# Feed-forward gate: silu and its scaling move from SBUF and GpSimd into PSUM and to VectorE

## What is computed

```python
def swiglu(x, w_in, w_out):
    gate, up = jnp.split(x @ w_in, 2, axis=-1)
    return (jax.nn.silu(gate) * up) @ w_out

x = x + 0.5 * swiglu(rms_norm(x, norm_g[l, 0]), ffn_w_in[l, 0], ffn_w_out[l, 0])
```

## Time and profile before

| | |
|---|---|
| three runs, median | 2074.32 us (2071.76 to 2074.66) |
| profiled execution, first to last instruction | 2071.8 us |
| profiled execution, its own time | not given apart from the span |
| TensorE busy | 2041.6 us, 99% |
| VectorE busy | 1329.3 us, 64% |
| ScalarE busy | 867.2 us, 42% |
| GpSimd busy | 1297.1 us, 63% |
| mean granted TensorE clock | 0.995 of full speed |

### The profile page before, as it was taken

The page is one execution under the profiler, slowest core; times in us unless marked ns, Lnnn a source line. Parts: engine busy times, 40 slices in busy tenths (PEclk is TensorE's granted clock), DMA queues, the critical chain, the costliest instruction groups (busy, mean ns, idle before and its releaser), DMA issues.

```text
span 2071.8 us, 41329 instructions
## 1 busy us (share of the span) xinstructions
PE 2041.6 (99%) x16420; PEld 1994.5 (96%) x16420; DVE 1329.3 (64%) x1873; ACT 867.2 (42%) x1651; POOL 1297.1 (63%) x999
## 2 busy tenths in 40 slices
PE   9999999999999999999999999999999999999998
PEld 8999999999989999999999999999998799999997
DVE  7861884425756882497578439844876678816853
ACT  6641662121574661364256226511432446505631
POOL 6775777654425676677767757765643267766773
PEclk9999999999999999999999999999999999999999
DMA  4321333122112232223123322333210232322231
GB/s 158 102 105 69 103 110 122 65 103 71 68 43 92 82 111 92 76 101 125 69 82 103 112 66 99 117 112 112 88 62 31 90 102 82 118 77 101 93 123 45
DMA packets 31702, 190.61 MB, mean 92 GB/s; under 512 B 3888, under 2 KB 6448, under 8 KB 13104
## 3 DMA queue, kind: packets, MB, share of 16 engines
q1 hardware_dynamic: 24192, 173.43, 24.3%
q10 hardware_dynamic: 7344, 14.89, 2.0%
HBM read 180.81 MB, written 7.50 MB: 91 GB/s over the span
## 4 chain that ended last, share of the span: by engine, by line
PE 52%; DVE 20%; POOL 10%; ACT 8%; issue 6%; DMA 2%; ACTq 0%; DVEq 0%; POOLq 0%; SPq 0%
PE ps L615 36%; PE ps L630 8%; DVE tg L2362 5%; POOL sil L526 4%; DVE tg L2359 4%; POOL ws L507 3%; DMA wraw<-in_wf_in 2%; POOL wl L573 2%; DVE a L2271 2%; DVE s L2300 2%; ACT sil L1761 2%; DVE ps L2280 2%; ACT ps L1692 1%; ACT ws L1725 1%; DVE ps L2338 1%
## 5 line engine op out<-in xcount | busy, mean ns | idle before, releaser
L690 PE MATMUL ps<-tt,ws 128*128 128x272 f32 x3840 | 526.2, 290 | 7.2 <-DVE ws L2304 6.4
L690 PEld LDWEIGHTS ps<-tt,ws 128*128 128x128 f32 x3840 | 500.0, 189 | 10.7 <-DVE ws L2304 7.3
L615 PE MATMUL ps<-a,wh 128*128 128x272 f32 x3028 | 500.3, 287 | 1.6 <-POOL wl L573 1.6
L573 POOL TENSOR_TENSOR wl<-wraw,wh 128x512 fp32r<-128x512 f32 (+1 forms) x351 | 475.2, 1376 | 12.7
L569 POOL TENSOR_SCALAR wh<-wraw 128x1024 fp32r<-128x1024 f32 (+2 forms) x152 | 167.7, 1103 | 471.2 <-PE ps L615 244.7
L615 PEld LDWEIGHTS ps<-a,wh 128*128 128x128 f32 x3028 | 423.6, 188 | 3.7 <-POOL wl L573 3.4
L690 PE MATMUL ps<-u,ws 128*128 128x272 f32 x2880 | 401.6, 288 | 1.1 <-DVE tg L2350 0.6
L507 POOL TENSOR_TENSOR ws<-wraw,ws 128x512 fp32r<-128x512 f32 x240 | 330.9, 1391 | 99.1 <-ACT ws L1700 55.6
L690 PEld LDWEIGHTS ps<-u,ws 128*128 128x128 f32 x2880 | 376.6, 188 | 2.4 <-issue 1.6
L615 PE MATMUL ps<-a,wl 128*128 128x272 f32 x1514 | 311.9, 287 | 0.0
L507 POOL TENSOR_TENSOR ws<-s,ws 128x512 fp32r<-128x512 f32 x160 | 209.0, 1306 | 142.3 <-ACT ws L1725 142.3
(11 more groups left out here) (391 smaller groups left out, 2929.4 us busy)
## 6 DMA issues: line engine op xcount, KB each, us to landing
wraw<-in_wf_in SPq DMA_DIRECT2D x87, 1024.0 KB, 4.8
wraw<-in_wf_out SPq DMA_DIRECT2D x32, 1408.0 KB, 6.0
wraw<-in_w_ab SPq DMA_DIRECT2D x12, 1024.0 KB, 4.8
wraw<-in_w_cd SPq DMA_DIRECT2D x10, 1024.0 KB, 4.9
wraw<-in_w_abo SPq DMA_DIRECT2D x8, 512.0 KB, 3.6
wraw<-in_w_cdo SPq DMA_DIRECT2D x8, 512.0 KB, 3.6
wraw<-in_w_bv SPq DMA_DIRECT2D x2, 1024.0 KB, 4.9
out_y<-yout ACTq DMA_DIRECT2D x14, 136.0 KB, 1.9
```

The lines of the kernel that those rows point to most:

```text
L573: piece = nc.gpsimd.tensor_tensor(wl[:, s, some], wraw[:, par_, s * K * P + some.start: s * K * P + some.stop], wh[:, s, some].bitcast(F32 ...
L615: last = nc.tensor.matmul(bank(b0 + 2 * s + half, 0, HT), w[:, s, k * P:(k + 1) * P], act_t[:, k0 + k, part, half * HT:(half + 1) * HT], s ...
L690: last = nc.tensor.matmul(bank(b, 0, HT), ws[weights][w][:, i * P:(i + 1) * P], moving[:, part], start=(start and i == 0 and w == 0 and pa ...
```

## The change

Silu is written by ScalarE into two banks of PSUM that its period no longer needs (banks 3 and 4 for b = 0, 0 and 1 for b = 1: the F and X bank of the period), not into `sil`. VectorE multiplies it there by `rstd` (`gate_scale`, in place) where GpSimd did so in SBUF, waits for its own completion (`link`), and `glu` reads the gate from PSUM. GpSimd's instruction is gone; so is VectorE's line 2392, whose place `gate_scale(end)` takes. The X bank is now in use until the last product, so `evac[0]` is given by that product instead of by ScalarE's copy, the copy gives a new semaphore `row_copied`, and the second output product waits for `evac[0]`. Each `glu` keeps its order: right half, C22 of the end period where there is one, left half. `link` (line 2114) adds a semaphore increment to an instruction and makes VectorE wait for it.

```diff
--- before.py
+++ after.py
@@ -360,8 +360,9 @@
         a21_in, w_sum, near_high, far_high = sem("a21_in"), sem("w_sum"), sem("near_high"), sem("far_high")
         sum_split, mix_split = sem("sum_split"), sem("mix_split")
         seven_done, t3_ready = sem("seven_done"), sem("t3_ready")
-        snap_ready, c_ready, silr_ready, snap_free = (
-            sem("snap_ready"), sem("c_ready"), sem("silr_ready"), sem("snap_free"))
+        snap_ready, c_ready, snap_free, row_copied = (
+            sem("snap_ready"), sem("c_ready"), sem("snap_free"), sem("row_copied"))
+        GATE_PAIR = [3, 0]
 
 
 
@@ -406,6 +407,7 @@
                 chains.append([Period(first + i, SEVENS * f + i - LEAD, i, DC, (hi - 1 - i) % 2, i == hi - 1)
                              for i in range(lo, hi)])
             SEQ.append(chains)
+        PAIR_OF = {(f, p.i): p.c for f in range(4) for chain in SEQ[f] for p in chain}
 
 
         ORDER, ORDER_END = ["P1", "P5", "P6", "P2", "P7"], ["P1", "P6", "P5", "P7", "P2"]
@@ -521,9 +523,6 @@
                     pool.wait_ge(far_high, 3 * p.q + 2)
                     pool.wait_ge(w_sum, 4 * p.q + 4)
                     low(p, A22, quarter(p, 3)).then_inc(w_split[1], 1)
-                    if last:
-                        pool.wait_ge(sil_done, FC * f + last.i + 1)
-                        nc.gpsimd.tensor_tensor(sil[:], sil[:], rstd[:], ALU.mult).then_inc(silr_ready, 1)
                     pool.wait_ge(far_high, 3 * p.q + 3)
                     low(p, S4, s34[:, 1, 0:p.K * P // 2]).then_inc(mix_split, 1)
 
@@ -902,6 +901,7 @@
 
                 _, c0, c1, _, K = STAGE[stage]
                 product(0, c0, K, a, act_ready, base, early=1)
+                pe.wait_ge(evac[0], c0)
                 product(1, c1, K, a, act_ready, base)
                 run(stage, a, act_ready, base, 1, hi)
 
@@ -1674,7 +1674,10 @@
 
             def glu_high(f, i):
 
-                act.wait_ge(glu_done, FC * f + i + 1)
+                if i < LEAD:
+                    act.wait_ge(glu_done, LEAD * f + i + 1)
+                else:
+                    act.wait_ge(evac[0], PAIR_OF[f, i] + 1)
                 nc.scalar.copy(a[:, slot(i), 0, :], tg[:, 1 + i % 2, :]).then_inc(act_high, 1)
 
             def seven_acts(f, g, before, between):
@@ -1745,20 +1748,21 @@
 
                 def snapshot7(p):
                     act.wait_ge(seven_done, sevenths(p, "P7"))
-                    act.wait_ge(evac[0], p.c)
+                    if p is p0:
+                        act.wait_ge(evac[0], p.c)
                     if p.q:
                         act.wait_ge(snap_free, p.q)
                     nc.scalar.copy(snap7[:], bank(X_BANK[p.b], 0, HT)).then_inc(snap_ready, 1)
 
                 def second_row(p):
                     act.wait_ge(prod_done[0], p.c + 1)
-                    act.wait_ge(evac[0], p.c)
                     act.wait_ge(act_ready, FC * f + p.i - 1)
-                    nc.scalar.copy(tg[:, 1 + p.i % 2, 0:HT], bank(X_BANK[p.b], 0, HT)).then_inc(evac[0], 1)
+                    nc.scalar.copy(tg[:, 1 + p.i % 2, 0:HT], bank(X_BANK[p.b], 0, HT)).then_inc(row_copied, 1)
 
                 def gate(p):
                     act.wait_ge(evac[1], p.c + 1)
-                    nc.scalar.activation(sil[:], tg[:, 0, :], ACT.Silu).then_inc(sil_done, 1)
+                    act.wait_ge(row_copied, p.q + 1)
+                    nc.scalar.activation(pair(GATE_PAIR[p.b]), halves(tg[:, 0, :]), ACT.Silu).then_inc(sil_done, 1)
 
                 high_a11(p0, None)
                 if between:
@@ -2352,14 +2356,18 @@
                         V.tensor_tensor(tg[:, 0, h1], bank(V_BANK, 0, HT), rstd[:, h1], ALU.mult)
                         V.tensor_tensor(tg[:, 0, h2], bank(F, 0, HT), rstd[:, h2], ALU.mult).then_inc(evac[1], 1)
 
+                def gate_scale(p):
+                    dve.wait_ge(sil_done, FC * f + p.i + 1)
+                    B = pair(GATE_PAIR[p.b])
+                    link(V.tensor_tensor(B, B, halves(rstd[:]), ALU.mult))
+
                 def glu(p, then=None):
-                    dve.wait_ge(evac[0], p.c + 1)
-                    dve.wait_ge(silr_ready, 20 * f + p.i - LEAD + 1)
-                    b = 1 + p.i % 2
-                    V.tensor_tensor(tg[:, b, h2], snap7[:], sil[:, h2], ALU.mult).then_inc(snap_free, 1)
+                    b, B = 1 + p.i % 2, GATE_PAIR[p.b]
+                    V.tensor_tensor(tg[:, b, h2], bank(B + 1, 0, HT), snap7[:], ALU.mult).then_inc(snap_free, 1)
                     if then:
                         c22(then)
-                    V.tensor_tensor(tg[:, b, h1], tg[:, b, h1], sil[:, h1], ALU.mult).then_inc(glu_done, 1)
+                    dve.wait_ge(row_copied, p.q + 1)
+                    V.tensor_tensor(tg[:, b, h1], bank(B, 0, HT), tg[:, b, h1], ALU.mult).then_inc(evac[0], 1)
 
                 for n, p in enumerate(seq):
                     last = seq[n - 1] if n else None
@@ -2380,6 +2388,7 @@
                         sum2(next_)
                         sum3(next_)
                     if last:
+                        gate_scale(last)
                         glu(last, p if p.end else None)
                     if next_:
                         sum4(next_)
@@ -2388,8 +2397,7 @@
                 glu_low(f, end.i - 1)
                 c12(end)
                 first_row(end)
-                dve.wait_ge(sil_done, FC * f + end.i + 1)
-                V.tensor_tensor(sil[:], sil[:], rstd[:], ALU.mult).then_inc(silr_ready, 1)
+                gate_scale(end)
                 glu(end)
                 glu_low(f, end.i)
```

## The result

Four runs of the kernel before, beside the changed one, took 2071.31 to 2074.66 us, median 2073.04. Four runs of the changed kernel took 2061.14, 2062.51, 2064.72 and 2064.83 us, median 2063.61. The ratio is 0.995 with a 95% interval of 0.9938 to 0.9962: by the medians the change makes the kernel 9.4 us faster, where 8.0 were forecast. A second set of five runs gave 2062.57 us beside 2073.02 of before, 10.5 us.

What follows compares the result with a forecast made beforehand. TensorE, busy 2041.6 of 2071.8 us, was taken as the bound, so only its waits could be won. Holes of 1.66, 2.07, 2.96, 0.88 and 0.44, together 8.0, came off the median 2074.3: 2066.3 us, range 2063.3 to 2071.0.

Steps and rivals of the forecast that it cites:

- The three kinds of holes: TensorE's late blocks at first chains' start (0.83 us each), in their last periods (0.53) and before the output projection (0.37).
- the second chains: Last period of these chains: one block 0.08 us late in three, 0.20 in two blocks of the fourth; 0.44 together.
- The wait ahead of the second block: In each first chain TensorE waits for VectorE's line 2304, 6.4 us in four waits; the change leaves it.
- The slack of the bank: The block waiting for the last gate product to release its bank starts at 122.12, with 2.0 us to spare.
- The holes that the change can close: Sum of TensorE's late starts in both kinds of chain and at the output projection: 8.0 us, 0.39%.
- the start of the first chain: Feed-forward calls 0 and 2: three blocks take 5.36 us, 0.83 over 4.53; counted two times, 1.66 us.
- the small starts in the middle periods: Single starts some 0.05 us late, worth 0.4 us, used only for the lower end of the range.
- Rival D: Clock falls to 1.2 GHz in calls 1 and 3: both gone or two more, 2063.7 or 2068.9 us; chance 0.10.
- the eight holes of the projection: Last block to output projection: TensorE waits for GpSimd's pieces of line 573, 8 x 0.37 = 2.96 us.
- The rival taken from the Trainium skill, VectorE: DVE Perf Modes, TRN2 errata: Gate products get no faster, VectorE stays late: gain 3.8 us, 2070.5; chance 0.14 together with the projection's holes staying.

## Why the prediction was right and wrong

**Right, by its steps.** The three kinds of holes closed as counted. Calls 0 and 2 were each to win 0.83 + 0.53 + 0.37 = 1.73 us and won 1.7 and 2.1; calls 1 and 3 were to win 0.9 and won 0.97 and 0.84; the second chains were to win 0.45 and 0.57 and won 0.47 to 0.52 and 0.61. The wait ahead of the second block stayed at 6.4. Products (0.43 to 0.44), scaling (0.725) and silu (629 ns instead of 660, within the 0.05 of the bounds) came as costed; GpSimd's pieces started at 130.6 (forecast 131.3) and ended at 134.6. The slack of the bank was 1.9 where 2.0 were counted.

**Wrong in size.** The forecast came out at 2066.3 us and the median at 2063.61, 2.7 lower. The gain was forecast at 8.0 and measured at 9.4 and 10.5. Three steps failed.
- "The holes that the change can close" counted the start of the first chain two times, for calls 0 and 2. Calls 1 and 3 have the same two early holes, which the clock falls of the traced execution had hidden. Each is worth 1.1 to 1.2 us more whenever the clock does not fall. So 8.0 should have been 8.0 to about 10.4, plus 0.4 for the small starts in the middle periods, which were named as a bound and not put in the sum; in the two first traces, where both calls fell, chains and starts gave 8.4.
- The 8.0 were taken from the median of three runs, 2074.32. Of these one lay in the lower cluster and two in the upper; with a fourth run the median was 2073.04. These 1.3 us come from which cluster the middle run lies in; the fall in the mixer, worth 2.8, is the one difference of about that size that the traces show.
- Rival D priced each fall in calls 1 and 3 at 1.3 us and two of them at 2.6. The slow stretch costs 1.45, near that, but the holes that it hides were put at nothing: before the change a chain with a fall lost no more than one without, after it 1.0 more. D also counted only these two falls; the one in the mixer is larger, stands outside the change, and its row was in the trace. With what D quoted from the Trainium skill, TensorE: Matmul & The Clock Gate, Part 1 (the window runs freely), the traces agree: waits of 0.81 and 0.82 us were followed by a fall in one execution and none in another. That is no proof of the rule.

**Right with the wrong reason.** The prediction put the eight holes of the projection down to GpSimd's instruction in its queue. Put back in that queue it opened none. And it took the faster products for an effect of the PSUM input alone; from SBUF they are as fast wherever no instruction of GpSimd runs beside them, and once VectorE no longer starts on GpSimd's signal the kernel is as fast too. In both cases it was the place in time that cost, not the place in memory or in the queue. The rival taken from the Trainium skill, VectorE: DVE Perf Modes, TRN2 errata (SBUF pairs cheaper than a PSUM source), would have needed the products to gain nothing in cost. Alone they show 0.43 to 0.44 us from either, which is neither the 0.34 estimated from its table for SBUF nor a penalty for PSUM; the 0.41 estimated for PSUM is near.

**Not seen beforehand.** VectorE was to fall to 1220 and fell to 1251 us. The low part of `a` (two SBUF inputs) now meets GpSimd's subtraction more often, as at 113.40, 1.48 us beside the 1.29 at 113.01; its mean went from 1233 to 1400 ns, 88 times, 14.7 of the 31 us. I did not break down the rest. No wait of TensorE names this line.

**Left open.** Why the clock falls in one execution and not in another; and whether the changed kernel meets fewer falls than before or only the same number, for which three traces of each are too few. With the two, the gain of 9.4 in one set and 10.5 in the other cannot be split further. Open is also whether GpSimd's instruction would cost anything without the signal if the gate lay in SBUF.

## What to carry to other kernels

When one engine's completion starts another's work, look at what the first does next. GpSimd and VectorE both read SBUF then, and the signal itself made them collide in all 80 periods. The 98 us of GpSimd's own time were worth nothing; the moment at which they released VectorE was worth some 10. A hole that is missing from a trace may be hidden by a slower stretch just ahead of it, so compare the same place in all repetitions and in a second trace before you count how often a repair pays. And sort the runs of before into their clusters before a gain is taken from their median.

## What the runs showed of the hardware

- A VectorE product of 128 x 272 in fp32 takes 0.43 to 0.44 us from two SBUF tiles and from one PSUM and one SBUF tile alike. From two SBUF tiles it takes 1.34 to 1.53 us when instructions of GpSimd (a subtraction takes 1.29 us alone) run beside it (line 2359, 80 times); with one input in PSUM it takes 0.44 beside them too (80 times).
- ScalarE's silu of 544 columns takes 629 ns into PSUM and 660 into SBUF.
- In one execution TensorE's clock goes to 1.2 GHz for 6.8 us, 2.6 us behind the end of a wait of 0.8 us, which costs 2.8 us, and in another not, with a wait of the same length in the same place.
- A fall to 1.2 GHz ahead of other waits hides them: it costs 1.45 us by itself, but over the chain about nothing in the kernel before and 1.0 us in the changed one.
- 98.8 us of added GpSimd work that reads and writes SBUF did not move the time where VectorE's products beside it had one input in PSUM.
